# State-space scan of a two-block decoder on one core: the running sums of all heads are made once and put on partitions, and a unit's rows are taken from them by products over 64 rows

## The chip, the cores and the metric

The kernel runs on one core of a Trainium2 chip. The metric is the device time of one execution in microseconds (us). A core has TensorE (PE in the profile; its weight loads are listed apart as PEld), VectorE (DVE), ScalarE (ACT), GpSimd (POOL, here used for DMA only) and SyncE (SP, which issues the weight loads). Each engine works through its own instructions in order and waits for the others on semaphores.

## The reference, cut to what matters

Two blocks of two layers each run over 512 tokens of width 1024. The first block holds sliding-window attention, a gated linear recurrence, a gated delta rule and a feed-forward part. The second block, which the change touches, holds a state-space branch, differential attention and cross attention. The change lies in the state-space scan of the second block, in both of its layers:

```
def _ssd_scan(xs, a, bm, cm):            # Q = 128 tokens a chunk, 32 heads, 4 groups
    a = a.reshape(Bsz, C, Q, G, R).transpose(0, 3, 4, 1, 2)
    a_cum = jnp.cumsum(a, axis=-1)
    lower = jnp.tril(jnp.ones((Q, Q), dtype=bool))
    seg = a_cum[..., :, None] - a_cum[..., None, :]
    decay = jnp.exp(jnp.where(lower, seg, -jnp.inf))
    y_diag = jnp.einsum('bcqgn,bcsgn,bgrcqs,bcsgrp->bcqgrp', cm, bm, decay, xs)
    ...
```

It is done twice, forward and over the flipped sequence, so that there are 64 head-directions. `a` is negative or zero, and `decay` of one head and chunk is a 128 x 128 matrix.

## The kernel before, in words

**Tiling.** All projections are products of the 512 tokens with 512 columns of weights, made as three fp32r products of high and low halves (line 570, the `main` work). The weights come through a ring of three buffers; ScalarE writes their high half (`sph`), VectorE their low half (`spl`), and TensorE waits for the low half. The state-space scan is one of a dozen side programs that are woven between these products.

**A unit of the scan.** `SSD` lists 32 units of a layer: a group g of eight heads, a chunk m of 128 tokens and a half q of the group, so a unit has four heads. For each unit and each of the two directions d, TensorE takes a PSUM bank and fills it with four 128 x 128 tiles, one a head, that hold the running sum of `a` at token t in every row, with -1e30 where the direction's mask forbids the pair. This is one "group" of this text: first a mask product over the whole bank (line 2138, `NFr`, fp32r, 128 rows, 512 columns), and then four fp32 products (line 2142). Each takes one column of `AA` (tokens on partitions, 64 head-directions beside one another), spread to 128 columns, as the stationary operand, and the triangle of ones `U` or `Lr` as the moving one; it sums over 128 tokens and so makes the running sum of one head, and gives it to all 128 output rows at once. There are 32 units x 2 directions = 64 groups a layer and 128 in all, with 512 such products. The trace shows two MATMUL records for one fp32 product.

**What follows a group.** ScalarE takes the exponential of the four tiles with the bias `BL` into `ES`; VectorE adds the two directions and multiplies by the scores; one unit later TensorE multiplies the result (`ES`) with `XS`, four products of 128 x 64 (line 103, "yd"). Line 103 is the helper `Tensor.mm`, line 109 its transpose.

**The sums themselves.** Long before the first group, `ssd_pe` makes the running sums and totals of all heads with tokens on partitions (bank "cum", 12 products with a stationary triangle or ones). `ssd_dve` copies them out as `NC` (negated) and `AL`, which give the biases and the decays of states.

**What sets the order.** `weave` runs first in a dry pass and writes a plan. It steps the main program by one tile (six products of line 570 for a 512-column block), and then up to three side steps that are due. The clock of this plan is `q.t`, which each product of TensorE advances by an assumed cost (0.22 for a product of line 2142), and the pair that a side step yields, such as `(1.5, 1.5)`, is the load assumed on VectorE and ScalarE, which sets when its next step is due. All engines then follow the same plan. `second_gates` names slots of the main program by which a side program must have come to a given step; the later stage `pass` (states between chunks, products of 128 x 512 on line 103) starts its second half after unit 18 of the scan, and must be over before the third column block of `z`.

Of the kernel before, what the change touches and what calls it, by code (L numbers as in the profile page):

```python
# [215 lines left out]
def bc(ap, axis, n):  # L216
    v = ap.unsqueeze(axis)
    shape = list(v.shape)
    shape[axis] = n
    return v.to_broadcast(shape)  # L220
# [65 lines left out]
def program(nc, T, out):  # L286
    ctx = ExitStack()
    with ctx:
# [16 lines left out]
        with nc.sbuf_tensor("arena_r", [128, ARENA], F32R) as ARr:  # L305
# [31 lines left out]
        at = Marks()  # L337
        bank_of, plans = {}, {}
        POOLS = dict(gemm=(0, 1, 2, 3), side=(4, 5, 6, 7), main=(0, 1), gdn=(2, 3), att=(4, 5), hgrn=(6, 7), xm=(2,), wout=(0, 1, 6, 7),
                     seg=(4, 5), yd=(6,), low=(4, 5), high=(6, 7), last=(7,),  # L340
# [4 lines left out]
        ident = cst[:, K_ID:K_ID + 128]  # L345
        U = cst[:, K_U:K_U + 128]
        Lr = cst[:, K_L:K_L + 128]
# [6 lines left out]
        def ar(off, *shape, of=None):  # L354
            n = 1
            for s in shape:
                n *= s
            assert off + n <= ARENA, (off, n)
            v = (AR if of is None else of)[:, off:off + n]
            if len(shape) == 2:  # L360
                v = v.rearrange("p (a b) -> p a b", a=shape[0])
            elif len(shape) == 3:
                v = v.rearrange("p (a b c) -> p a b c", a=shape[0], b=shape[1])
            return v

        def take(pe, key, pool="side"):

            i = POOLS[pool][lane[pool] % len(POOLS[pool])]
            lane[pool] += 1
            pe.wait_ge(at["free", held_by[i]] if i in held_by else None)  # L370
            held_by[i] = key
            bank_of[key] = banks[i]
            return banks[i]
# [1540 lines left out]
        R4 = 20480  # L1914
# [9 lines left out]
        XW = [cst[:, K_AM + 512 * i:K_AM + 512 * (i + 1)] for i in range(2)]  # L1924
        ES = [ar(R4 + 1024 * i, 2, 4, 128) for i in range(2)]
        AA = ar(R4 + 2688, 4, 64)
        NC = ar(R4 + 2944, 4, 64)
        AL = ar(R4 + 2432, 4, 64)
        BL = ar(R4 + 2176, 4, 64)
# [181 lines left out]
        def ssd_pe(pe, l):  # L2111
            yield (2, 3)
            bank = take(pe, ("cum", l), "seg")
            pe.wait_ge(at["aa", l])
            for m in range(4):
                pe.mm(bank[:, m * 64:m * 64 + 32], [(U, AA[:, m, 0:32])])
                pe.mm(bank[:, m * 64 + 32:m * 64 + 64], [(Lr, AA[:, m, 32:64])])
                at["cum2", l] = pe.mm(bank[:, 256 + m * 64:256 + m * 64 + 64], [(ones, AA[:, m, :])])
            yield (2.5, 2.4)
            scores_pe(pe, l, 0)  # L2120
            yield (0.4, 1)
            by = None
            for n in range(34):
                for d, tri in enumerate((U, Lr)):
                    if n > 1 and d == 0:
                        pg, pm, pq = SSD[n - 2]
                        if pq == 0:
                            by = take(pe, ("yd", l, n - 2), "yd")
                        pe.wait_ge(at["em", l, n - 2], at["xt", l, pg])
                        for h in range(4):  # L2130
                            c0 = 256 * pq + 64 * h
                            at["yd", l, n - 2] = pe.mm(by[:, c0:c0 + 64], [(ES[n % 2][:, 0, h, :], XS[:, pg, pm, c0:c0 + 64])])
                    if n < 32:
                        g, m, q = SSD[n]
                        h0 = 32 * d + 8 * g + 4 * q
                        bank = take(pe, ("seg", l, n, d), "seg")
                        pe.wait_ge(at["aa", l], at["nfr"])
                        pe.e.matmul(bank.rearrange("p (h t) -> p h t", h=4), NFr[0][:, :], bc(NFr[1 + d][:, :], 1, 4),  # L2138
                                    start=True, stop=False)
                        pe.t += 0.23  # L2140
                        for h in range(4):
                            ins = pe.e.matmul(bank[:, h * 128:(h + 1) * 128],  # L2142
                                              AA[:, m, h0 + h:h0 + h + 1].to_broadcast([128, 128]), tri, start=False, stop=h == 3)
                            pe.t += 0.22
                        ins.then_inc(*pe.done.up())
                        at["seg", l, n, d] = pe.now()
                    if d == 1 and n in (4, 12, 20):
                        scores_pe(pe, l, n // 8 + 1)
                    yield (1.5, 1.5)

        def scores_pe(pe, l, g):

            bank = take(pe, ("cbt", l, g), "last")
            pe.wait_ge(*[at["xbc", l, i] for i in range(16, 24)])
            for m in range(4):
                ms = slice(m * 128, (m + 1) * 128)
                at["cbt", l, g] = pe.mm(bank[:, ms], [(BT[:, g, ms], CTt[:, g, ms])])

        def scores_act(a, l, g):
            a.wait_ge(at["cbt", l, g], *[at["xbc", l, i] for i in range(10, 16) if g > 1])  # L2160
            at["cb", l, g] = at["free", ("cbt", l, g)] = a.cp(
                Y[:, g, :, 0:128], bank_of["cbt", l, g].rearrange("p (m c) -> p m c", m=4), par=True)

        def ssd_act(a, l):
# [4 lines left out]
            a.act(u, u, ACT.Exp, scale=-1.0)  # L2169
            a.act(NC[:, 0, :], r2[:, R2["alog"]:R2["alog"] + 64], ACT.Exp)  # L2170
            at["dsp", l] = a.act(u, u, ACT.Ln, bias=1.0)
# [7 lines left out]
            a.wait_ge(at["bl", l])  # L2179
            at["ac", l] = a.act(NC, NC, ACT.Exp, scale=-1.0)  # L2180
            scores_act(a, l, 0)
# [16 lines left out]
        def ssd_dve(v, l):  # L2198
            u = AL.rearrange("p a b -> p (a b)")
            v.wait_ge(at["dsp", l])  # L2200
            v.stt(dtf, dtf, 0.0, u, ALU.max, ALU.add)
            at["aa", l] = v.stt(AA, DT, -1.0, bc(NC[:, 0, :], 1, 4), ALU.mult, ALU.mult)
            yield
            bank = bank_of["cum", l]
            v.wait_ge(at["cum2", l])
            v.ts(NC, bank[:, 0:256].rearrange("p (a b) -> p a b", a=4), -1.0, None, ALU.mult)
            at["free", ("cum", l)] = v.cp(AL, bank[:, 256:512].rearrange("p (a b) -> p a b", a=4), par=True)
            v.ts(BL, DT, 1e-38, None, ALU.max, par=True)
            for d in range(2):
                hs = slice(32 * d, 32 * d + 32)  # L2210
                at["wd0", l] = v.tt(WD[d], AL[:, WDm[d], hs], NC[:, WDm[d], hs], ALU.add, par=d > 0)
            v.wait_ge(at["bln", l])
            at["bl", l] = v.tt(BL, BL, NC, ALU.add)
            yield
            v.wait_ge(at["wd1", l])
            for d in range(2):
                hs = slice(32 * d, 32 * d + 32)
                v.tt(WD[d], WD[d], DT[:, WDm[d], hs], ALU.mult, par=d > 0)
            yield
            for n in range(34):  # L2220
                if 0 < n < 33:
                    pg, pm, pq = SSD[n - 1]
                    E2 = ES[(n - 1) % 2]
                    v.wait_ge(at["se", l, n - 1, 1], at["cb", l, pg])
                    v.tt(E2[:, 0], E2[:, 0], E2[:, 1], ALU.add, par=True)
                    at["em", l, n - 1] = v.tt(E2[:, 0, :, :], E2[:, 0, :, :], bc(Y[:, pg, pm, 0:128], 1, 4), ALU.mult)
                yield
                if n > 1:
                    pg, pm, pq = SSD[n - 2]
                    if pq == 1:  # L2230
                        xg, yg = XS[:, pg, pm, :], Y[:, pg, pm, :]
                        v.wait_ge(at["xt", l, pg])
                        v.tt(r3(yg), r3(xg), bc(r2[:, R2["skip"] + 8 * pg:R2["skip"] + 8 * pg + 8], 2, 64), ALU.mult)
                        v.wait_ge(at["yd", l, n - 2])
                        at["free", ("yd", l, n - 3)] = v.tt(yg, yg, bank_of["yd", l, n - 3][:, :], ALU.add)
                yield
# [528 lines left out]
        def second_sides(q, l):  # L2765
# [7 lines left out]
            for g in range(4):  # L2773
# [8 lines left out]
            empty = iter(())  # L2782
            return [("conv0", conv(q, l, 0), (), cs[0]), ("conv1", conv(q, l, 1), (), cs[1]),
                    ("ssd", side(q, pe=ssd_pe, dve=ssd_dve, act=ssd_act)(q, l), (), ssd),
                    ("pass", side(q, pe=pass_pe, dve=pass_dve, act=pass_act)(q, l), (), passes),
                    ("gated", side(q, pe=gated_pe, dve=gated_dve, act=gated_act)(q, l), (), gated),
# [219 lines left out]
```

## Time and profile before

| | |
|---|---|
| median of 3 runs | 4436.93 us (4436.51 to 4437.48) |
| the profiled execution, own time | 4433.45 us |
| its span | 4431.7 us |
| PE busy (matmuls) | 4051.1 us, 91% of the span |
| DVE busy | 2573.7 us, 58% |
| ACT busy | 1639.0 us, 37% |
| mean granted TensorE clock | 0.945 of full speed |
| share of PE in the chain that ended last | 75%, of which line 570 alone 55% |
| groups of the scan | 64 in each layer, between 2070.2 and 2447 us and between 3310.4 and 3686 us |

Busy time is the sum of the times in which an engine executed something. Matmuls overlap one another in TensorE (a record runs from its start to its last result), so that the time which a matmul costs is read from the distance between starts, not from its duration. The chain is followed back from the last instruction, at each step to what released it.

### The profile page before, as it was taken

What the parts mean: (1) busy time and instruction counts of PE and PEld (TensorE: products, weight loads), DVE (VectorE), ACT (ScalarE), POOL (GpSimd) and SP (SyncE); (2) the same over time, 40 slices, a digit from 0 to 9 for tenths busy, and PEclk for the clock granted to TensorE, in tenths of its full rate; (3) what the DMA queues carried; (4) which work ended last, traced back from release to release, by engine and by line L of the source; (5) the groups of instructions that cost most, each with busy time, mean ns of one, the idle gap of its engine ahead of it and who ended that gap; (6) DMA issues with size and microseconds to landing.
All of it is one profiled execution on the core that took longest, in us unless ns stands there. A gap on an engine that the chain in (4) does not pass through costs nothing.

```text
span 4431.7 us, 51774 instructions
## 1 busy us (share of the span) xinstructions
PE 4051.1 (91%) x20660; PEld 3326.6 (75%) x20660; DVE 2573.7 (58%) x4060; ACT 1639.0 (37%) x2880; POOL 107.7 (2%) x199
## 2 busy tenths in 40 slices
PE   5878979988879899999999999999899999999998
PEld 4757868867659778888888777767778787777776
DVE  6775455554675332346666744676566667445865
ACT  2343232233443232333434233453344343334532
POOL 0000000000000000000000000000000000000000
PEclk9978889999979799989999999999899999999999
DMA  6402135633202133323231233133242312231233
GB/s 219 148 15 67 44 119 189 191 124 96 72 10 77 58 95 96 98 93 105 81 105 58 81 91 91 53 108 119 70 132 78 109 60 84 81 91 62 78 105 121
DMA packets 216641, 417.93 MB, mean 94 GB/s; under 512 B 16384, under 2 KB 61472, under 8 KB 214608
## 3 DMA queue, kind: packets, MB, share of 16 engines
q1 hardware_dynamic: 197584, 335.12, 24.4%
q0 software_dynamic: 18816, 79.49, 5.2%
q8 instruction: 163, 2.67, 0.2%
q14 instruction: 78, 0.64, 0.0%
HBM read 378.89 MB, written 35.67 MB: 94 GB/s over the span
## 4 chain that ended last, share of the span: by engine, by line
PE 75%; DVE 15%; ACT 6%; DMA 2%; issue 2%; DVEq 0%; SPq 0%; ACTq 0%; POOLq 0%
PE ps L570 55%; PE ps L103 14%; DVE arena L120 4%; ACT arena L191 3%; PE ps L109 3%; DVE arena L135 3%; DVE spl L120 3%; PE ps L2142 2%; ACT sph L191 1%; DMA ring<-in_ada_w 1%; DVE sm L141 1%; DVE HF L120 1%; DVE X L120 1%; PE ps L2138 1%; DVE arena L129 0%
## 5 line engine op out<-in xcount | busy, mean ns | idle before, releaser
L120 DVE TENSOR_TENSOR spl<-ring,sph 128x1024 fp32r<-128x1024 f32 (+2 forms) x556 | 651.6, 1179 | 834.7 <-ACT sph L191 833.3
L191 ACT ACTIVATE sph<-ring 128x1024 fp32r<-128x1024 f32 (+2 forms) x556 | 562.2, 1021 | 878.6 <-PE ps L570 668.2
L570 PE MATMUL ps<-sph,HTh 128*128 128x512 f32 (+3 forms) x1728 | 685.5, 397 | 10.7 <-ACT sm L191 5.4
L570 PE MATMUL ps<-spl,HTh 128*128 128x512 f32 (+3 forms) x1728 | 638.6, 370 | 0.0
L570 PE MATMUL ps<-sph,HTl 128*128 128x512 f32 (+3 forms) x1728 | 637.5, 369 | 0.0
L191 ACT ACTIVATE arena<-ps 128x512 f32<-128x512 f32 (+2 forms) x574 | 316.9, 564 | 778.6 <-PE ps L570 479.2
L570 PE MATMUL ps<-HTh,sph 128*128 128x512 f32 x1376 | 548.4, 399 | 23.1 <-DVE spl L120 16.0
L570 PE MATMUL ps<-HTh,spl 128*128 128x512 f32 x1376 | 540.1, 393 | 0.0
L570 PE MATMUL ps<-HTl,sph 128*128 128x512 f32 x1376 | 540.0, 392 | 0.0
L103 PE MATMUL ps<-arena 64*128 64x128 f32 (+7 forms) x2328 | 410.5, 368 | 55.7 <-ACT arena L191 22.3
L570 PE MATMUL ps<-sph 128*128 128x512 f32 x992 | 402.4, 406 | 8.8 <-DVE spl L120 8.7
L570 PEld LDWEIGHTS ps<-sph,HTh 128*128 128x128 f32 x1728 | 339.2, 196 | 83.7 <-issue 32.9
L570 PE MATMUL ps<-sph,spl 128*128 128x512 f32 x992 | 391.8, 395 | 0.0
L103 PEld LDWEIGHTS ps<-arena 64*128 64x128 f32 (+2 forms) x2328 | 296.2, 211 | 127.2 <-issue 28.9
L570 PE MATMUL ps<-spl,sph 128*128 128x512 f32 x992 | 390.5, 394 | 0.0
L570 PEld LDWEIGHTS ps<-sph,HTl 128*128 128x128 f32 x1728 | 339.5, 196 | 62.9 <-issue 18.8
L570 PEld LDWEIGHTS ps<-spl,HTh 128*128 128x128 f32 x1728 | 338.4, 196 | 53.3
L570 PEld LDWEIGHTS ps<-HTh,sph 128*128 128x128 f32 x1376 | 261.4, 190 | 78.6 <-DVE spl L120 22.7
L570 PEld LDWEIGHTS ps<-HTh,spl 128*128 128x128 f32 x1376 | 260.9, 190 | 55.7
L570 PEld LDWEIGHTS ps<-HTl,sph 128*128 128x128 f32 x1376 | 261.3, 190 | 53.1 <-issue 1.0
L109 PE MATMUL ps<-cst,arena 128*128 128x128 f32 x1160 | 186.7, 298 | 117.9 <-ACT arena L191 73.2
L109 PEld LDWEIGHTS ps<-cst,arena 128*128 128x128 f32 x1160 | 146.4, 153 | 168.0 <-ACT arena L191 71.0
(195 smaller groups left out, 5293.6 us busy)
## 6 DMA issues: line engine op xcount, KB each, us to landing
ring<-in_w_in SPq DMA_DIRECT2D x264, 512.0 KB, 3.7
ring<-in_ada_w SPq DMA_DIRECT2D x96, 512.0 KB, 4.4
ring<-in_w_down SPq DMA_DIRECT2D x44, 512.0 KB, 3.3
ring<-in_w_gate SPq DMA_DIRECT2D x40, 512.0 KB, 4.2
ring<-in_w_up SPq DMA_DIRECT2D x40, 512.0 KB, 4.6
ring<-in_w_mem SPq DMA_DIRECT2D x32, 512.0 KB, 3.4
ring<-in_w_out SPq DMA_DIRECT2D x32, 512.0 KB, 3.7
ring<-in_w_br_ssd SPq DMA_DIRECT2D x32, 512.0 KB, 3.8
```

What stands on the lines that cost most here:

```text
L103: ins = self.e.matmul(o, l, r, start=i == 0, stop=stop)
L109: self.e.transpose(o, i, ident).then_inc(*self.done.up())
L120: self.e.tensor_tensor(o, a, b, op).then_inc(*self.done.up())
L135: self.e.scalar_tensor_tensor(out=o, in0=a, scalar=s1, in1=b, op0=op0, op1=op1).then_inc(*self.done.up())
L141: self.e.tensor_reduce(o, a, AX, op).then_inc(*self.done.up())
L191: self.e.activation(o, a, f, **kw).then_inc(*self.done.up())
L570: ins = pe.e.matmul(o, l, r, start=k0 == 0 and i == 0 and not b.pairs, stop=k0 + b.ks == b.kt and i == 3 * b.ks - 1 and (c0 > 0 or not b.p ...
L2138: pe.e.matmul(bank.rearrange("p (h t) -> p h t", h=4), NFr[0][:, :], bc(NFr[1 + d][:, :], 1, 4), start=True, stop=False)
L2142: ins = pe.e.matmul(bank[:, h * 128:(h + 1) * 128], AA[:, m, h0 + h:h0 + h + 1].to_broadcast([128, 128]), tri, start=False, stop=h == 3)
```

## The change: what it does

After the bank "cum", a second bank "cumt" is filled once a layer by eight fp32 products. Their stationary operand is `AA[:, m, 32 d : 32 d + 32]` (128 tokens x 32 heads), their moving operand the triangle, so the running sums come out with heads on partitions and tokens along the row. Chunks 0 and 1 lie on partitions 0 to 63 (heads of both directions), chunks 2 and 3 on partitions 64 to 127. VectorE copies them to `CUMT`, 128 x 256, which takes the place of `AA` in SBUF. In a group the mask product stays. The four fp32 products change their operands: stationary is now one column of 64 rows of the identity, spread to 128 columns, and moving 64 rows by 128 columns of `CUMT`, so each picks one head's row and gives it to all 128 output rows. Their number and output are the same; they sum over 64 rows and not over 128. The plan's assumed cost of one is 0.11 and no longer 0.22, and the yield after the sums is (2.9, 2.4).

```diff
+        CUMT = ar(R4 + 2688, 256)
...
                 at["cum2", l] = pe.mm(bank[:, 256 + m * 64:256 + m * 64 + 64], [(ones, AA[:, m, :])])
-            yield (2.5, 2.4)
+            bank = take(pe, ("cumt", l), "seg")
+            for m in range(4):
+                for d, tri in enumerate((U, Lr)):
+                    r = 64 * (m // 2) + 32 * d
+                    at["cumt_t", l] = pe.mm(bank[r:r + 32, m % 2 * 128:m % 2 * 128 + 128], [(AA[:, m, 32 * d:32 * d + 32], tri)])
+            yield (2.9, 2.4)
...
                         bank = take(pe, ("seg", l, n, d), "seg")
-                        pe.wait_ge(at["aa", l], at["nfr"])
+                        rows = slice(64 * (m // 2), 64 * (m // 2) + 64)
+                        pe.wait_ge(at["cumt", l], at["nfr"])
                         pe.e.matmul(bank.rearrange("p (h t) -> p h t", h=4), NFr[0][:, :], bc(NFr[1 + d][:, :], 1, 4),
                                     start=True, stop=False)
                         pe.t += 0.23
                         for h in range(4):
-                            ins = pe.e.matmul(bank[:, h * 128:(h + 1) * 128],
-                                              AA[:, m, h0 + h:h0 + h + 1].to_broadcast([128, 128]), tri, start=False, stop=h == 3)
-                            pe.t += 0.22
+                            one = 64 * (m // 2) + h0 + h
+                            ins = pe.e.matmul(bank[:, h * 128:(h + 1) * 128], ident[rows, one:one + 1].to_broadcast([64, 128]),
+                                              CUMT[rows, m % 2 * 128:m % 2 * 128 + 128], start=False, stop=h == 3)
+                            pe.t += 0.11
                         ins.then_inc(*pe.done.up())
...
             at["free", ("cum", l)] = v.cp(AL, bank[:, 256:512].rearrange("p (a b) -> p a b", a=4), par=True)
+            v.wait_ge(at["cumt_t", l])
+            at["cumt", l] = at["free", ("cumt", l)] = v.cp(CUMT, bank_of["cumt", l][:, 0:256], par=True)
             v.ts(BL, DT, 1e-38, None, ALU.max, par=True)
```

TensorE, at the sums of the first layer of the second block, before:

```order
6494 L103 MATMUL ps<-arena,cst 128x64
6495 L103 MATMUL ps<-arena,cst 128x32 x2
6496 L103 MATMUL ps<-arena,cst 128x64
6497 L570 MATMUL ps<-HTh,sph 128x512
```

and now:

```order
6494 L103 MATMUL ps<-arena,cst 128x64
6495 L103 MATMUL ps<-arena,cst 128x32 x2
6496 L103 MATMUL ps<-arena,cst 128x64
6497 L103 MATMUL ps<-cst,arena 32x128 x8
6498 L570 MATMUL ps<-HTh,sph 128x512
```

The eight products of the new bank stand directly behind the old twelve, before the main products go on.

TensorE, at unit 25 of the same layer, before (L2138 is a group's mask product, L2142 its four fp32 products, `ps<-arena 128x64 x4` the yd products of an earlier unit):

```order
L103 MATMUL ps<-cst,arena 128x512
L103 MATMUL ps<-arena 128x64 x4
L2138 MATMUL ps<-nfr 128x512
L2142 MATMUL ps<-cst,arena 128x128 x4
L570 MATMUL ps<-sph,HTh 128x512
L570 MATMUL ps<-sph,HTl 128x512
L570 MATMUL ps<-spl,HTh 128x512
L570 MATMUL ps<-sph,HTh 128x512
L570 MATMUL ps<-sph,HTl 128x512
L570 MATMUL ps<-spl,HTh 128x512
L2138 MATMUL ps<-nfr 128x512
L2142 MATMUL ps<-cst,arena 128x128 x4
```

and the same unit now (the lines are L2145 and L2150):

```order
L103 MATMUL ps<-arena 128x64 x4
L2145 MATMUL ps<-nfr 128x512
L2150 MATMUL ps<-arena,cst 128x128 x4
L570 MATMUL ps<-sph,HTh 128x512
L570 MATMUL ps<-sph,HTl 128x512
L570 MATMUL ps<-spl,HTh 128x512
L570 MATMUL ps<-sph,HTh 128x512
L570 MATMUL ps<-sph,HTl 128x512
L570 MATMUL ps<-spl,HTh 128x512
L570 MATMUL ps<-sph,HTh 128x512
L570 MATMUL ps<-sph,HTl 128x512
L570 MATMUL ps<-spl,HTh 128x512
```

Between two groups there now stand more products of the main work. The first four groups of a layer stand within 6 products of line 570 of their old places, the first of unit 25 48 later, the last one 78 later, and the last product of `pass` 60 later; the total numbers of L570 products (13440) and of groups (128) are unchanged. A group of the new order is followed by a product of line 570 in 100 cases and by another product of line 103 in 28.

## Rows read from the trace of the kernel before

**Rows 1.** The page: all engines, and the granted clock by 40 slices.

```profile
PE 4051.1 (91%) x20660; PEld 3326.6 (75%) x20660; DVE 2573.7 (58%) x4060; ACT 1639.0 (37%) x2880; POOL 107.7 (2%) x199
PEclk9978889999979799989999999999899999999999
```

**Rows 2.** Windows over the scan's two stages: us, busy time of each engine, granted clock.

```profile
2060.00:2450.00 390.00, 375.51 (x2016) 316.44 (x2015) 246.51 (x341) 164.94 (x384) 17.35 (x32) 0.99 0.26 82
3300.00:3690.00 390.00, 375.17 (x2021) 315.72 (x2020) 248.13 (x343) 165.09 (x384) 17.35 (x32) 0.99 0.26 82
```

**Rows 3.** Waits of TensorE in 2060 to 2450: total us, times, longest.

```profile
PE ps L109 <- ACT arena L191: 6.7, 6, 1.5
PE ps L103 <- ACT arena L191: 5.2, 3, 3.7
PE ps L103 <- DVE X L135: 1.2, 1, 1.2
```

**Rows 4.** Waits of ScalarE in 2060 to 2450.

```profile
ACT arena L191 <- PE ps L2142: 102.7, 57, 4.5
```

**Rows 5.** Timeline of TensorE, one group: start, us, instruction (rows*columns used), count.

```profile
2070.16 0.39 PE L2138 MATMUL ps<-nfr 128*128 128x512 f32 x1
2070.39 1.05 PE L2142 MATMUL ps<-cst,arena 128*128 128x128 f32 x8
2071.19 0.48 PE L570 MATMUL ps<-sph,HTh 128*128 128x512 f32 x1
2071.51 0.39 PE L570 MATMUL ps<-sph,HTl 128*128 128x512 f32 x1
```

**Rows 6.** Groups of instructions, whole run: the group's fp32 products.

```profile
L2142 PE MATMUL ps<-cst,arena 128*128 128x128 f32 x1024 | 137.4, 278 | 0.0
```

**Rows 7.** Timeline of TensorE, attention scores: four products over the same 64 rows.

```profile
180.13 0.39 PE L570 MATMUL ps<-HTl,sph 128*128 128x512 f32 x1
180.35 0.39 PE L570 MATMUL ps<-HTh,spl 128*128 128x512 f32 x1
180.67 1.16 PE L103 MATMUL ps<-arena 64*128 64x128 f32 x8
181.76 0.50 PE L570 MATMUL ps<-HTh,sph 128*128 128x512 f32 x1
182.10 0.39 PE L570 MATMUL ps<-HTl,sph 128*128 128x512 f32 x1
```

**Rows 8.** Timeline of TensorE: products over 128 and over 64 rows in turn.

```profile
385.24 1.52 PE L103 MATMUL ps<-arena 128*128 128x64 f32 x8
```

**Rows 9.** Timeline of TensorE: four yd products and what follows.

```profile
2164.66 1.00 PE L103 MATMUL ps<-arena 128*128 128x64 f32 x8
2165.46 0.48 PE L2138 MATMUL ps<-nfr 128*128 128x512 f32 x1
```

**Rows 10.** Timeline of TensorE: a group at the lower clock.

```profile
2123.98 0.77 PE L2138 MATMUL ps<-nfr 128*128 128x512 f32 x1
2124.55 1.91 PE L2142 MATMUL ps<-cst,arena 128*128 128x128 f32 x8
2126.11 0.77 PE L570 MATMUL ps<-sph,HTh 128*128 128x512 f32 x1
2126.68 0.63 PE L570 MATMUL ps<-sph,HTl 128*128 128x512 f32 x1
```

**Rows 11.** Timeline of TensorE, the sums of all heads, and of VectorE's copies.

```profile
1980.36 2.79 PE L103 MATMUL ps<-arena,cst 128*128 128x32 f32 x24
1982.95 0.47 PE L570 MATMUL ps<-HTh,sph 128*128 128x512 f32 x1
...
1983.52 0.41 DVE L153 COPY arena<-ps 128x256 f32<-128x256 f32 x1
```

**Rows 12.** Timeline of TensorE, recurrence: products over rows 0-63 and 64-127 in turn.

```profile
1285.53 1.16 PE L103 MATMUL ps<-arena 64*128 64x128 f32 x16
1286.62 0.55 PE L109 MATMUL ps<-cst,HF 128*128 128x128 f32 x3
```

More of the change, by code:

```diff
@@ L2123, in ssd_pe @@
             for n in range(34):
-                for d, tri in enumerate((U, Lr)):
+                for d in range(2):
                     if n > 1 and d == 0:
```

## The prediction

> **What bounds the kernel now.** I read the page's busy times first, then windows over the two stages in which the scan's groups run, then TensorE's waits there, then its timeline. TensorE is busy in 91% of the span, and the granted clock is near full in most slices [rows 1]. In the two stages of 390 us it is busy 375.5 and 375.2 us, 96%, at a clock of 0.99, with VectorE at 247 us and ScalarE at 165 [rows 2]. Its three largest kinds of wait in the first stage add up to 13.1 us, of which 6.7 are six waits for ScalarE's copies out of the one bank of the transposes [rows 3]. So in these stages the end is set by how long TensorE needs for its own instructions, and 128 groups of five products are a part of that. ScalarE on its side waits 102.7 us for the groups' products [rows 4]: it has room, and a group that comes later by some tenths of a us costs it nothing. The question is thus one of TensorE's pace: what do four fp32 products cost over 128 rows, and what over 64?
>
> **The group before.** Since matmuls overlap, I take distances between starts. In [rows 5] the mask product starts at 2070.16 and the second main product behind the group at 2071.51. These 1.35 us hold the mask product (0.23), the eight records of the four products, and one main product (0.23; the main products stand 0.23 apart). Eight records are left 0.90 us, 0.11 each. The 1024 records over the whole run have 137.4 us of busy time [rows 6], 0.13 each, since some of a record's end is counted as well; 1024 x 0.112 = 115 us is what they occupy.
>
> **The group after, step by step.** The number of records stays 1024, so the saving could come only from the pace of one. The trace has this very form: in the attention scores of the first block four fp32 products with 64 rows, 128 stationary and 128 moving columns, all on the same 64 partitions, stand between main products of 512 columns [rows 7]. From the start of the last main product before them (180.35) to the start of the second one behind (182.10) are 1.75 us, for a product of 512 columns, the eight records and another product of 512 columns: the same content as the 1.35 us of [rows 5]. Eight records over 64 rows thus cost 0.40 us more than eight over 128 rows, not less. Where it goes is seen in the starts: 180.35 to 180.67 are 0.32 for a product that elsewhere takes 0.23, and 181.76 to 182.10 are 0.34. The record group itself lasts 1.16 and not 1.05 us. So the pace within is the same, and both changes of the number of rows, from 128 to 64 and back, cost about 0.20 us each.
>
> Every group changes twice, because its mask product stays at 128 rows and what follows is 128 rows too. 100 groups are followed by a main product: 100 x 0.40 = 40.0 us. 28 are followed by another fp32 product. For that change the nearest row is [rows 8], where products over 128 and 64 rows alternate in pairs of records: eight records last 1.52 us, with three changes among them, against 1.00 us for eight records of the same size without one [rows 9], so a change costs (1.52 - 1.00) / 3 = 0.17 us. 28 x (0.20 + 0.17) = 10.4 us. About three groups fall where the clock is granted at half (2.70 us for what takes 1.35 otherwise, [rows 10]), and pay their changes double: 1.2 us. Together 51.6 us. With 0.17 for every change it would be 128 x 0.34 = 43.5 us, which I keep as the low end of this term.
>
> The Trainium skill, TensorEngine Tiling (Array Packing), Key Properties, says that a change of the tiling mode, and not merely of the tile, drains TensorE. The trace agrees: a change costs 0.17 to 0.20 us. That page of the Trainium skill has no price; by it the sum is the one above, and without such a drain the 51.6 us would fall away.
>
> **The bank of sums.** Added to TensorE are 16 records a layer, directly behind 24 records that take 1980.36 to 1982.95, 0.11 each [rows 11]. Their outputs go to quarters of 32 partitions, a form that the trace does not have. From above: the pace of 0.11 and two changes, 16 x 0.11 + 0.4 = 2.2 us. From below: neighbours run side by side as in [rows 12], where 16 records over alternating halves last from 1285.53 to 1286.62, 0.07 each, so 1.1 + 0.2 = 1.3 us. I take 1.8, since neighbours here alternate as well but the form is another: 3.5 us for two layers, all on the path, because main products stand behind. VectorE's additional copy is 0.41 us [rows 11], twice. It stands before the biases `BL`, but the first group comes 85 us later, and VectorE is busy in only 63% of such a stage: nothing. The groups' new wait for this copy is met for the same reason.
>
> **The order.** The plan believes a group 0.44 us cheaper, while TensorE will need 0.40 more. It puts more main products between groups, up to 78 of them by the last. That takes nothing away and adds nothing to TensorE, and gives ScalarE and VectorE more time for each group. The last `pass` product comes 60 main products later, 60 x 0.23 = 14 us, still before the gate. Cost: 0, with up to 10 us if VectorE is then late for the columns of `z`; and below nothing, by what is absorbed: while TensorE waits for others, its additional time is free. Of the 13.1 us of [rows 3] the 6.7 follow from TensorE's own transposes and move along with them. The other 6.4 can shrink, in both layers 13, and I take 5 of them off.
>
> **Sum.** 51.6 + 3.5 - 5 = 50 us. The profiled execution took 4433.45 us, so 4483.5; the median of the runs shown lies 3.5 us above it, so 4487. The low end is 43.5 + 2.6 - 13 = 33 us, 4470; the high end 51.6 + 4.4 + 10 = 66 us, 4503.
>
> **Rivals.**
> *Half the rows cost half.* Then 512 products would save 1024 x 0.056 = 57 us, and if changes of rows were free, the time would be 4437 - 57 + 3.5 = 4383, faster. For it speaks that 16 records of alternating halves take little longer than 8 [rows 7, 12], which may also be what the plan's 0.11 was read from. Against it: in [rows 12] neighbours lie on different halves, and here all four products of a group, both directions and four units in a row lie on one half. This is the case that ends on the other side; it decides from the point where a record takes less than 0.06 us. I give it 0.03. With the changes still paid it gives 4437 - 57 + 55 = 4435, no change: 0.02.
> The Trainium skill, TensorEngine Tiling (Array Packing), Theoretical Speedup, promises up to twofold for 64 rows. The same skill, TensorE: Matmul & The Clock Gate, Why this matters for your kernels, says that a single product over few rows takes as long as over 128 and that the gain is concurrency. Here [rows 7] side with the second.
> *The changes are hidden.* If the long mask product in front covered the loading of the 64-row operand, only the bank of sums would be left: 4440, within 0.2%. Against it: in [rows 7] a product of 512 columns stands in front too, and covers nothing. 0.04.
> *A new wait adds to it.* VectorE or ScalarE is late for `z` or for a group that now stands elsewhere, more than 10 us beyond my sum: above 4503. For it: the pass stage is moved by 14 us. Against it: TensorE has never waited more than 3.7 us there [rows 3]. 0.06.
> *More is absorbed than can be named*, for instance because the new order removes the waits for transposes: 4446 to 4464. 0.05.
>
> **How the numbers follow.** My forecast has 0.80, with 4464 to 4503 around it, and this is also the range: it leaves 0.20 outside at most. This kernel's measurement can tell some 0.2%, 9 us, from no change. Faster by more than that: 0.03, the first rival. Within: 0.02 + 0.04 = 0.06. Slower: the rest, 0.91. I put the value at 4487 and not at the range's middle because the group's 0.40 is read from a form that agrees in all sizes.
>
> **What would show it.** Records of line 2150 read 64*128 64x128 and stand 0.11 apart; the main product in front of the mask keeps its 0.23, but the mask product takes 0.32 until the first record, the first record 0.2, and the main product behind the group 0.34. TensorE's busy time in the stage of the scan rises, its idle time does not. The sixteen records behind the sums take 1.3 to 2.2 us. The prediction is wrong if the records of line 2150 stand 0.06 apart, if the distance of 1.35 us around a group has not become about 1.75, or if TensorE's idle time in the two stages falls or rises by more than 10 us.

## The result, and the profile after

The changed kernel takes 4473.9 us (median of 4 runs, 4465.5 to 4480.1), the kernel before 4437.2 us (4436.5 to 4443.4) beside it: a ratio of 1.0081 [1.0062, 1.0101], 36.7 us slower. In a later comparison it was 4476.5 against 4436.9 us, 1.0086 [1.0072, 1.01]. The forecast was +50 us and 4487: the sign, the mechanism and the range held, the sum was 13 us too high.

First the page of the profiled execution (4465.52 us, span 4463.7).

```profile
PE 4100.7 (92%) x20692; PEld 3331.8 (75%) x20692; DVE 2573.8 (58%) x4062; ACT 1639.1 (37%) x2880; POOL 107.4 (2%) x199
PEclk9878889999879799999999999999899999999999
```

Against [rows 1] TensorE has 49.6 us more of busy time and 32 more records, VectorE two more instructions and no more time. The stretches to compare are those from a layer's sums to the next layer's sums and to the end, since the change acts only there. Windows of the kernel before (us, busy time of each engine, granted clock, DMA share, GB/s):

```profile
1980.36:3223.31 1242.95, 1184.92 (x5750) 956.50 (x5749) 766.80 (x1206) 496.17 (x909) 44.85 (x81) 0.97 0.28 89
3223.31:4431.67 1208.36, 1144.33 (x5579) 919.64 (x5577) 748.48 (x1164) 478.38 (x882) 43.24 (x78) 0.98 0.28 89
```

and of the changed one, with the stage of 390 us that answers to the first of [rows 2] ahead of them:

```profile
2060.00:2450.00 390.00, 380.04 (x1908) 303.59 (x1907) 228.52 (x314) 155.79 (x354) 17.30 (x32) 0.99 0.27 83
1975.64:3237.41 1261.77, 1209.51 (x5766) 957.97 (x5764) 767.65 (x1207) 496.52 (x909) 44.74 (x81) 0.97 0.28 88
3237.41:4463.73 1226.32, 1166.37 (x5595) 919.72 (x5593) 748.78 (x1164) 478.27 (x882) 43.15 (x78) 0.99 0.28 88
```

The two layers became 18.8 and 18.0 us longer, together 36.8. That this is also the difference of the medians is in part luck: the two profiled executions themselves lie 32.1 us apart, since in this one, the fastest of its four, the first sums start at 1975.64 and not at 1980.36, 4.7 us early, before the change has done anything. In the traces of all kernels here these first sums start between 1975.6 and 1986.0, so that traces are compared layer by layer. A second trace of the changed kernel (4467.64 us) has layers of 1261.8 and 1227.2 us, within 1 us of these. Both traces are of executions near the low end of 4465.5 to 4480.1; what the longer ones add is in no trace. TensorE's busy time rose by 24.6 and 22.0 us. What it has beside that, length less busy time, fell from 58.0 and 64.0 us to 52.3 and 60.0: 9.8 us less idle. So the sum has two parts: TensorE works 47 us longer and waits 10 us less.

TensorE's timeline of one group, which answers to [rows 5] (start, length, instruction):

```profile
2072.95 0.39 PE L570 MATMUL ps<-HTh,spl 128*128 128x512 f32 x1
2073.18 0.39 PE L2145 MATMUL ps<-nfr 128*128 128x512 f32 x1
2073.50 1.15 PE L2150 MATMUL ps<-arena,cst 64*128 64x128 f32 x8
2074.58 0.50 PE L570 MATMUL ps<-HTh,sph 128*128 128x512 f32 x1
2074.92 0.40 PE L570 MATMUL ps<-HTl,sph 128*128 128x512 f32 x1
```

The main product in front keeps its 0.23. From the mask product to the second main product behind the group it is 1.74 us, where [rows 5] have 1.35 and [rows 7] 1.75. The mask product now takes 0.32 until the first record (before 0.23), the eight records 1.08 until the main product (before 0.80), and that one 0.34 (before 0.32). Stretches of the timeline that are so narrow that they start with the second record, and with the eighth, show where the 0.28 of the records lies; in the changed kernel

```profile
2073.71 0.38 PE L2150 MATMUL ps<-arena,cst 64*128 64x128 f32 x2
2074.38 0.27 PE L2150 MATMUL ps<-arena,cst 64*128 64x128 f32 x1
```

and before, where the eighth starts at

```profile
2071.16 0.28 PE L2142 MATMUL ps<-cst,arena 128*128 128x128 f32 x1
```

The first record takes 0.21 until the second, the six between take 0.67 (2073.71 to 2074.38), 0.11 each as before, and the eighth takes 0.20 until the main product, where before it was 0.03. Over half as many rows a record is no faster.

The weight loads show what goes missing. TensorE's loading side in the changed kernel:

```profile
2072.96 0.19 PEld L2145 LDWEIGHTS ps<-nfr 128*128 128x128 f32 x1
2073.50 0.96 PEld L2150 LDWEIGHTS ps<-arena,cst 64*128 64x128 f32 x8 [0.35 <-issue]
2074.58 0.19 PEld L570 LDWEIGHTS ps<-HTh,sph 128*128 128x128 f32 x1
```

and before:

```profile
2069.94 0.19 PEld L2138 LDWEIGHTS ps<-nfr 128*128 128x128 f32 x1
2070.16 1.08 PEld L2142 LDWEIGHTS ps<-cst,arena 128*128 128x128 f32 x8
2071.17 0.19 PEld L570 LDWEIGHTS ps<-sph,HTh 128*128 128x128 f32 x1
```

A load normally runs beside the product in front of its own: before, the first load of the group starts with the mask product, 0.23 us ahead of the product that uses it (2070.39). In the changed kernel it starts at 2073.50, with its own product, after the loading side has stood 0.35 us. One line's summary has this 128 times, 40.4 us in all:

```profile
L2150 PEld LDWEIGHTS ps<-arena,cst x1024: 182/187/335, 2066.5 to 3737.2; 64*128 64x128 f32 x171
  issue: 40.4, 128
```

On the way back the loading side stands as well: the group's loads end at 2074.46 and the main product's starts at 2074.58. Before, the main product's load starts at 2071.17, with the eighth record (2071.16).

Last the waits of TensorE in 2060 to 2450, against [rows 3]:

```profile
PE ps L109 <- ACT arena L191: 6.7, 6, 1.5
PE ps L103 <- ACT arena L191: 2.1, 3, 0.7
PE ps L103 <- DVE X L135: 1.2, 1, 1.2
```

The longest wait of the stage, 3.7 us, has become 0.7. Nothing waits for VectorE's new copy.

### The profile page after: what moved, and what is told of

It is laid out like the page before. It is cut to its first block, busy times and chain, and to the rows that moved or that the text cites. A ratio compares the mean times of both kernels' runs of the same rounds, so it can differ in the third digit from the quotient of the medians.

```text
span 4463.7 us, 51843 instructions
## 1 busy us (share of the span) xinstructions
PE 4100.7 (92%) x20692; PEld 3331.8 (75%) x20692; DVE 2573.8 (58%) x4062; ACT 1639.1 (37%) x2880; POOL 107.4 (2%) x199
## 4 chain that ended last, share of the span: by engine, by line
PE 77%; DVE 13%; ACT 5%; DMA 2%; issue 2%; DVEq 0%; SPq 0%; ACTq 0%; POOLq 0%
PE ps L570 56%; PE ps L103 14%; DVE arena L120 3%; PE ps L2150 3%; PE ps L109 3%; ACT arena L191 3%; DVE arena L135 2%; DVE spl L120 2%; DMA ring<-in_ada_w 1%; ACT sph L191 1%; DVE sm L141 1%; DVE X L120 1%; DVE HF L120 1%; PE ps L2145 1%; ACT L191 0%
## 5 line engine op out<-in xcount | busy, mean ns | idle before, releaser
L570 PE MATMUL ps<-sph,HTh 128*128 128x512 f32 (+3 forms) x1728 | 688.8, 399 | 7.9 <-ACT sm L191 5.0
L570 PE MATMUL ps<-spl,HTh 128*128 128x512 f32 (+3 forms) x1728 | 639.6, 370 | 0.0
L570 PE MATMUL ps<-sph,HTl 128*128 128x512 f32 (+3 forms) x1728 | 638.0, 369 | 0.0
L570 PE MATMUL ps<-HTh,sph 128*128 128x512 f32 x1376 | 550.4, 400 | 22.8 <-DVE spl L120 16.0
L570 PE MATMUL ps<-HTl,sph 128*128 128x512 f32 x1376 | 540.8, 393 | 0.0
L570 PE MATMUL ps<-HTh,spl 128*128 128x512 f32 x1376 | 540.7, 393 | 0.0
L570 PE MATMUL ps<-sph 128*128 128x512 f32 x992 | 402.0, 405 | 9.6 <-DVE spl L120 9.6
L570 PEld LDWEIGHTS ps<-sph,HTh 128*128 128x128 f32 x1728 | 339.3, 196 | 89.9 <-issue 33.9
L570 PE MATMUL ps<-sph,spl 128*128 128x512 f32 x992 | 391.3, 394 | 0.0
L570 PE MATMUL ps<-spl,sph 128*128 128x512 f32 x992 | 390.0, 393 | 0.0
L570 PEld LDWEIGHTS ps<-sph,HTl 128*128 128x128 f32 x1728 | 339.9, 197 | 63.9 <-issue 19.6
L570 PEld LDWEIGHTS ps<-spl,HTh 128*128 128x128 f32 x1728 | 339.2, 196 | 53.2
L570 PEld LDWEIGHTS ps<-HTh,sph 128*128 128x128 f32 x1376 | 261.6, 190 | 83.2 <-DVE spl L120 22.3
L570 PEld LDWEIGHTS ps<-HTh,spl 128*128 128x128 f32 x1376 | 261.3, 190 | 56.1
L570 PEld LDWEIGHTS ps<-HTl,sph 128*128 128x128 f32 x1376 | 261.8, 190 | 53.3 <-issue 1.0
L120 DVE TENSOR_TENSOR arena<-arena 128x512 f32<-128x512 f32 (+4 forms) x412 | 224.1, 564 | 87.6 <-ACT arena L191 77.5
```

The costliest lines, as they stand in the source:

```text
L120: self.e.tensor_tensor(o, a, b, op).then_inc(*self.done.up())
L570: ins = pe.e.matmul(o, l, r, start=k0 == 0 and i == 0 and not b.pairs, stop=k0 + b.ks == b.kt and i == 3 * b.ks - 1 and (c0 > 0 or not b.p ...
```

## The experiments

The theories. *The rows:* the loss is the change between 128 and 64 rows around each group, and the new order gives some of it back. *The records:* the picks themselves, their operands or the bank of sums, are dearer than the old products. *The order:* the new order is what costs or gives. The first four kernels below ran beside the same runs of the kernel before (4437.15 us).

**The picks over all 128 rows.** From the changed kernel; one column of the identity over 128 rows picks the same head, so the number of products, the bank of sums and the plan stay.

```diff
-    ident[rows, one:one + 1].to_broadcast([64, 128]), CUMT[rows, m % 2 * 128:m % 2 * 128 + 128]
+    ident[:, one:one + 1].to_broadcast([128, 128]), CUMT[:, m % 2 * 128:m % 2 * 128 + 128]
```

> The changed kernel with one difference: the four products of a group sum over all 128 rows of the identity's column and of the transposed sums (the other half's rows are picked with zero). Same operands, same plan, same order, but no change of the number of rows. Theory (two changes of rows a group cost 0.39 us): the group falls from 1.74 to 1.35 us, 128 x 0.385 = 49 us off the changed kernel's 4474, so 4425, 12 us under the kernel before, since the plan's order lets 10 us less idle time on TensorE and only 1.5 us are added. Rival (the picking products or their operands are themselves slower): stays at about 4474. Rival (the order is what costs): 4474 too.

Measured: 4421.3 us (8 runs), 0.9968 [0.9958, 0.9979]: 52.6 us below the changed kernel (55.2 by its later median). The timeline of a group:

```profile
2154.12 0.39 PE L570 MATMUL ps<-HTh,spl 128*128 128x512 f32 x1
2154.35 0.39 PE L2145 MATMUL ps<-nfr 128*128 128x512 f32 x1
2154.58 1.05 PE L2150 MATMUL ps<-arena,cst 128*128 128x128 f32 x8
2155.39 0.48 PE L570 MATMUL ps<-HTh,sph 128*128 128x512 f32 x1
2155.70 0.39 PE L570 MATMUL ps<-HTl,sph 128*128 128x512 f32 x1
```

The mask product is back at 0.23, and from it to the second main product behind the group it is 1.35 again. Twice as many rows, nothing else changed, and 52.6 / 128 = 0.41 us a group are gone. This excludes the records: operands and bank are the same. A small part of the 52.6 us is clock: summed over the trace, 86.7 us of the two layers have the lower of TensorE's two clock levels here and 97.1 us in the changed kernel, and 10.4 us less at half speed are worth 5.2. The 0.39 of the timeline gives 50 us for 128 groups.

**The order alone.** The kernel before, with the changed kernel's numbers in the plan; TensorE's instructions then stand in exactly the changed kernel's order, the bank of sums aside. (The yield alone moves nothing; the 0.11 does.)

```diff
-            yield (2.5, 2.4)
+            yield (2.9, 2.4)
...
-                            pe.t += 0.22
+                            pe.t += 0.11
```

> The kernel before with nothing but the plan's numbers changed (0.11 for a product, 2.9 after the sums), which gives the changed kernel's order. Theory: the order by itself is worth minus 10 us of TensorE's idle time, 4427, group distance 1.35 us. Rival (order costs time, by later pass steps): above 4445.

Measured: 4419.6 us (5 runs), 0.9963 [0.995, 0.9975]: 17.5 us less. The order alone makes the kernel before faster, though not one instruction is cheaper. Its windows:

```profile
1985.95:3220.54 1234.59, 1181.62 (x5750) 954.73 (x5748) 766.91 (x1206) 496.24 (x909) 44.69 (x81) 0.98 0.29 90
3220.54:4420.08 1199.54, 1140.78 (x5579) 917.95 (x5577) 748.18 (x1163) 478.23 (x882) 43.12 (x78) 0.99 0.29 90
```

The layers are 8.4 and 8.8 us shorter than before. Idle time is 53.0 and 58.8 us, 10.3 less in all; busy time fell by 3.3 and 3.6 with the same instructions, and the granted clock of both stretches is up by 0.01, so a little more of the work ran at the upper of the two levels (1.2 and 2.4 GHz). Summed over the trace, the lower level has 104.4 us of the two layers before and 90.8 us here: 13.6 us less at half speed are worth 6.8 us, the whole of the busy time that went. Of the idle time, the waits of line 103 for ScalarE fell from 24.0 to 18.1 us in the two layers, and its waits for VectorE's line 120 from 2.4 us to none. The longest wait that went, before, and the mask product behind it:

```profile
2203.22 1.15 PE L103 MATMUL ps<-arena 128*128 128x64 f32 x8 [3.69 <-ACT arena L191]
2204.13 0.77 PE L2138 MATMUL ps<-nfr 128*128 128x512 f32 x1
```

and with the new order:

```profile
2211.95 1.10 PE L103 MATMUL ps<-arena 128*128 128x64 f32 x8 [0.69 <-ACT arena L191]
2212.87 0.47 PE L2138 MATMUL ps<-nfr 128*128 128x512 f32 x1
```

Behind the long wait the mask product lasts 0.77, as in [rows 10] at the lower level; behind the short one 0.47. The second layer shows the same pair: 4.04 us and 0.77, 0.69 us and 0.47. The long waits thus go together with a part of the lost clock. They are not its only occasion: the changed kernel has a stretch at the lower level shortly behind its 0.69 us wait in the first layer too.

**The old order around the new picks.** The changed kernel with the plan's old numbers (and the bank's products taken out of the plan's clock), so that TensorE's order is that of before.

```diff
+                    pe.t -= 128 / 596
-            yield (2.9, 2.4)
+            yield (2.5, 2.4)
...
-                            pe.t += 0.11
+                            pe.t += 0.22
```

> The changed kernel's products in exactly the order of the kernel before (assumed cost back at 0.22, the yield at 2.5). Theory: 4437 + 49 for the changes of rows + 1.5 for the bank of sums = 4488, and TensorE's idle time as before. Rival (the new order is what made it slower): near 4440.

Measured: 4492.6 us (4 runs), 1.0123 [1.0109, 1.0137]: +55.5 us (48 to 61 by the interval), where the forecast's first two terms are 51.6 + 3.5 = 55.1. The 3.7 us wait is back, and the idle time of the two layers is 120.3 us, against 122.1 before. Not all of the 55.5 is the groups': the lower level has 117.3 us of the two layers, 12.9 more than before, so that some 6 us are clock, by the same reckoning as above. And the parts add up: 55.5 - 17.5 = 38.0, against 36.7 and 39.6 measured for the change.

**Alternating halves.** The sums of the two directions lie on different halves of the partitions, and both directions of a unit are issued together: two mask products, then eight products in turn from either half, each direction into its own bank.

```diff
-                    r = 64 * (m // 2) + 32 * d
+                    r = 64 * d + 32 * (m // 2)
...
-                    if n < 32:
+                    if n < 32 and d == 0:
...
+                        for h, e in ((h, e) for h in range(4) for e in range(2)):
+                            r0 = 64 * e
+                            one = r0 + 32 * (m // 2) + 8 * g + 4 * q + h
```

> Direction 0 on partitions 0 to 63 and direction 1 on 64 to 127 (sums laid out so), both directions of a unit issued together: two mask products, then eight 64-row products that alternate between the halves, each direction in its own PSUM bank. Theory: one change in and out a unit and not two (64 x 0.385 = 25 us less than the changed kernel) and neighbours side by side, 0.056 us a record and not 0.112 (1024 x 0.056 = 57 us less): 4474 - 82 = 4392. Rival (no overlap here, since the spread identity or the accumulation on the mask holds them apart): 4474 - 25 = 4449.

Measured: 4396.1 us (4 runs), 0.9909 [0.9896, 0.9923]: the best version, 77.8 us below the changed kernel and 41 below the one before. Not all of the 41 belong to the halves: beside the kernel with picks over 128 rows, which has the same new numbers in the plan, it is 25 us. A pair of groups on TensorE:

```profile
2139.59 0.71 PE L2144 MATMUL ps<-nfr 128*128 128x512 f32 x2
2140.24 1.16 PE L2150 MATMUL ps<-arena,cst 64*128 64x128 f32 x16
2141.33 0.50 PE L570 MATMUL ps<-HTh,sph 128*128 128x512 f32 x1
2141.67 0.39 PE L570 MATMUL ps<-HTl,sph 128*128 128x512 f32 x1
```

Sixteen records last 1.09 us, as long as eight in the changed kernel (1.08). The gain is not the fewer changes of rows alone, as the next shows.

**One change for two groups, on one half.** As the last, but both directions of a unit on the same half, one after the other.

```diff
+                        for h, e in ((h, e) for e in range(2) for h in range(4)):
+                            r0 = 64 * (m // 2)
+                            one = r0 + 32 * e + 8 * g + 4 * q + h
```

> The changed kernel's layout (both directions of a chunk on the same 64 partitions), but both directions of a unit issued together: two mask products, then eight 64-row products, all on one half. So there are 64 pairs of changes of rows in place of 128, and no neighbours side by side. Theory (a pair of changes costs 0.39 us, a record 0.11): 64 x 0.39 = 25 us under the changed kernel's 4474, 4449; the stretch from the second mask to the second product behind takes 0.23 + 16 x 0.112 + 0.4 + 0.23 us = 2.65. Rival (what made the halves fast was the issuing together and not the overlap): 4396, as with the halves.

Measured: 4456.8 us (5 runs) beside 4435.5 before, 1.0047 [1.0033, 1.0061]: some 17 to 20 us below the changed kernel, where 25 were expected. The same place:

```profile
2141.83 0.71 PE L2144 MATMUL ps<-nfr 128*128 128x512 f32 x2
2142.48 2.05 PE L2150 MATMUL ps<-arena,cst 64*128 64x128 f32 x16
2144.45 0.50 PE L570 MATMUL ps<-HTh,sph 128*128 128x512 f32 x1
2144.79 0.40 PE L570 MATMUL ps<-HTl,sph 128*128 128x512 f32 x1
...
1980.89:3232.34 1251.45, 1196.45 (x5766) 956.35 (x5764) 766.14 (x1207) 493.21 (x909) 44.69 (x81) 0.97 0.29 89
3232.34:4452.47 1220.13, 1159.43 (x5595) 921.67 (x5593) 747.70 (x1164) 475.45 (x882) 43.11 (x78) 0.98 0.28 88
```

The sixteen records last 1.97 us and not 1.09: 0.88 x 64 = 56 us for all pairs, and the two kernels lie 60.7 us apart, 57 expected. The missing 5 to 8 us: the idle time is 55.0 and 60.7 us, 3.5 more than in the changed kernel; busy time fell by 13.1 us in the first layer but by only 6.9 in the second. The clock accounts for that: the first layer has 64.9 us of the lower level in both kernels, the second 46.2 us here and 32.2 in the changed kernel, and 14.0 us more at half speed cost 7.0. What made the clock fall there is not shown.

Between these two kernels one thing more differs than the halves. In the alternating one, neighbouring products also go to different banks, here four in a row go to one. Different banks alone do not let full-height products overlap: of the two mask products in front, each into its own bank, the second starts some 0.3 us behind the first, as late as any. But 64 rows of one half into alternating banks were not run.

**How far the order can be pushed.** The order depends on what the plan believes. With 0.04 in place of 0.11 more main products stand between groups. The kernel before:

```diff
-                            pe.t += 0.22
+                            pe.t += 0.04
```

> The kernel before with the assumed cost of a group's product at 0.04 in place of 0.22 (0.11 gave 4420). TensorE's real work is unchanged; the groups are spread wider still, the last one of a layer 120 main products later and not 78. Theory (wider spacing lets the waits for ScalarE and VectorE fall away, and most of them are gone at 0.11): 4415 to 4422, idle time of TensorE in a scan layer 53 and 40 us as at 0.11. Rival (later pass steps begin to cost): above 4430.

Measured: 4430.5 us (11 runs), 0.9988 [0.9979, 0.9997]. My theory, that less belief is better, missed; the rival held, by half a us. Its idle time is 56.4 and 62.4 us, 7 more than with 0.11. The waits named above are as short, but another kind, which the order with 0.11 does not have in either layer, stands in both:

```profile
PE ps L103 <- DVE arena L120: 3.0, 2, 1.5
```

These are 6.0 of the 7 us: with the groups this far apart line 103 waits for VectorE. The same step on the kernel with alternating halves:

```diff
-                            pe.t += 0.11
+                            pe.t += 0.04
```

> The version with the two halves side by side (4396), with the assumed cost of a product at 0.04 and not 0.11, so that groups stand wider apart. It still shows one wait of 2.3 us of TensorE for ScalarE in each scan layer. Theory: that wait goes, 2 to 5 us a layer, so 4387 to 4393. Rival: the order has nothing left to give, 4396.

Measured: 4405.4 us (5 runs), 0.9927 [0.9914, 0.9939]. Missed too: the wait of 2.3 us for ScalarE became 1.2, and the time rose by 9 us. In the first layer the same kind of wait for VectorE adds up to 3.5 us.

**Between the two.** 0.16, on the alternating halves and on the kernel before, and the changed kernel once more.

```diff
-                            pe.t += 0.11
+                            pe.t += 0.16
```

> The halves version (4396) with the assumed cost of a product at 0.16 in place of 0.11, so that the groups stand a little closer, still wider than in the kernel before. Theory (the order has an optimum near 0.11, where the waits of TensorE are few and the last pass steps are not yet late): within 6 us of 4396. Rival (closer is better, since 0.04 was worse by 9 us): 4388 or less.

Measured: 4397.0 us (4 runs), 0.9908 [0.9895, 0.9921], no different from 0.11.

```diff
-                            pe.t += 0.22
+                            pe.t += 0.16
```

> The kernel before with the assumed cost at 0.16 (0.22 gave 4437, 0.11 gave 4420, 0.04 gave 4430). Theory (what goes is the 3.7 us wait in front of the yd products at 2199 us and its like, and that depends on the groups near there, which at 0.16 stand 24 to 30 products later just as at 0.11): 4422 to 4428. Rival (the gain comes from the second half, where 0.16 moves groups by 24 and not 78): 4432 or more.

Measured: 4430.7 us (12 runs), 0.9987 [0.9979, 0.9996], between both expectations. Its profile still has a long wait:

```profile
PE ps L103 <- ACT arena L191: 4.7, 3, 3.2
```

Its idle time is 117.2 us in the two layers, 4.9 less than before, and its 107.3 us at the lower level are no fewer.

On the kernel before the beliefs 0.22, 0.16, 0.11 and 0.04 thus give 4437, 4431, 4420 and 4431 us: a narrow best place, not a slope. With alternating halves, 0.16 and 0.11 give the same and 0.04 is 9 us worse.

> The changed kernel once more, beside the kernel before on the same chip as the others of this call, since its four runs lay 15 us apart. Both theories: the median again between 4466 and 4480.

Measured, with the changed kernel unaltered: 4476.5 us (4 runs), 1.0086 [1.0072, 1.01].

## Why the prediction was right, and where its sum was off

*The group's 0.40 us.* Right in kind and size. Read from [rows 7], a form equal in all sizes, it came out as 0.39 in the timeline, with the surplus in the places named: 0.09 on the mask product, 0.10 on the first record (0.21, forecast 0.2) and 0.17 on the last. As a whole it is 55.5 us less 1.4 for the bank, 54.1, with the old order, and 52.6 in the comparison over 128 rows; 51.6 were forecast. A part of both is clock: 128 x 0.39 are 50. The low end, 43.5 by the 0.17 of [rows 8] for all changes, is too low.

The Trainium skill, TensorEngine Tiling (Array Packing), Key Properties, which has a change of the tiling mode drain TensorE, agrees with the loading side's 128 stops and with the 0.20 us between the last record and the next product; the price is only in the rows. The Trainium skill's promise of up to twofold, in TensorEngine Tiling (Array Packing), Theoretical Speedup, is nearly met here between neighbours on different halves (and in different banks), and not at all on one half: on one half, 16 records over 64 rows take 1.97 us; on alternating halves 1.09.

*The bank of sums.* Mis-sized. 1.8 us a layer were forecast, from bounds of 1.3 and 2.2.

```profile
1975.64 2.79 PE L103 MATMUL ps<-arena,cst 128*128 128x32 f32 x24
1978.36 0.66 PE L103 MATMUL ps<-cst,arena 128*32 128x128 f32 x16
1978.94 0.50 PE L570 MATMUL ps<-HTh,sph 128*128 128x512 f32 x1
```

From the sums to the next main product it is 3.30 us, where [rows 11] have 2.59: 0.7 us a layer, below my low bound. Sixteen records last 0.58 us. I had taken the pace of two halves side by side, [rows 12]; these outputs lie on four quarters. A narrow stretch of the same timeline,

```profile
1978.36 0.33 PE L103 MATMUL ps<-cst,arena 128*32 128x128 f32 x4
```

shows four records of which each lasts 0.30 and all four together 0.33: they run side by side. VectorE's copies, the new one among them,

```profile
1978.81 0.85 DVE L153 COPY arena<-ps 128x256 f32<-128x256 f32 x2
```

are done by 1979.66, and no wait for them appears: nothing, as said. In the sum this is 2 us of the 13.

*The order.* This is the step that failed, though the time stayed inside the range. It said that the plan's new number "takes nothing away and adds nothing to TensorE", with up to 10 us for a late `z`, and took 5 us off for absorbed idle time. Measured alone it is worth 17.5 us. The reasoning about absorption was the wrong one: idle time did not shrink because the groups became longer, since with the longer groups in the old order next to nothing was absorbed (120.3 us idle against 122.1, and +55.5 against 55.1). It shrank because other work stands between ScalarE's copies and the products that need them, which works on the unchanged kernel as well. Of the 17.5 us, 10.3 are idle time and 6.9 busy time that went with 13.6 us less at the lower clock. The first was inside my own range of 0 to 13 but put down to another cause; the second I did not have, although [rows 10] show what the lower level does to a group: twice the time. The longest wait, the 3.7 of [rows 3], I had counted among those that can shrink; the six waits of together 6.7 us stayed, as said. Term by term, too little was taken off for the order (5 us and not 17.5), too much put on for the bank (3.5 and not 1.4), and too little for the groups (51.6 and not 54.1): 12.5 + 2.1 - 2.5 = 12 of the 13 us.

*The signs.* The prediction named what would show it wrong. The record's pace (0.11), the distance around a group (1.74) and the places of the surplus came as named. TensorE's idle time in the two stages of 390 us fell from 29.3 to 19.9 us, 9.4, just under the limit of 10: the sign all but spoke against its account of the order. The sixteen records behind the sums, forecast at 1.3 to 2.2 us, took 0.58.

*The rivals.* "Half the rows cost half" is excluded by the 0.11 of a record on one half, and shown true of neighbours on different halves. "The changes are hidden" is excluded by the 0.32 of the mask product and the 1.74 around the group. "A new wait" did not appear: TensorE's waits of [rows 3] only became shorter. "More is absorbed" described the direction of the miss, and its clause on the order names the cause, at 17.5 us in place of the 5 I had taken off; for its times of 4446 to 4464 it would have needed 28 to 46.

What stays open: some 2 us of the 10.3 of idle time that the order saved; what makes the granted clock fall in one order and not in another, beyond the two long waits; and whether the overlap needs the other half, the other bank or both, since one half into alternating banks and two halves into the same bank were not tried. On the kernel before, 0.04 is 11 us slower than 0.11 by the medians and 6 us by the two layers of the traces; the other 5 are in no trace.

## What to carry to other kernels

In this kernel an fp32 product over 64 rows costs TensorE as long as one over 128, and each switch between the two forms costs some 0.2 us; it paid only where neighbours lay on the other half, with a group of eight products to carry two switches. When an edit also changes a number that a scheduler reads, measure that number alone on the old kernel first: here it hid a third of the loss, and of the 41 us by which the best version beats the kernel before some 16 came with the new numbers before any halves alternated (4421 against 4437). Such a number is worth a sweep of its own: here the best was half the true cost, and at a fifth of it most of the gain was gone.

## What the runs showed of the hardware that was not expected

- Sixteen fp32 records into four column quarters (128 rows, 32 stationary and 128 moving columns) last 0.58 us; the same number over alternating halves of rows, each half into its own bank (128 stationary columns), 1.09; on one half 1.97.
- In the timeline above, the first record after a change of rows loads its weights only when it starts itself; the loading side stood before such a record 128 times of 128, 0.32 us on average.
- An order with not one cheaper instruction lowered TensorE's busy time by 6.9 us: 90.8 us of the two layers at the lower clock where before it was 104.4.
